# A hybrid attention and MLP block on one core: first MLP product by Strassen's rule in 256-token tiles, out-projection and second MLP product token-major

## What is computed

```python
x = x + merged @ w_out[layer]                 # 2048 x 2048
h2 = rms_norm(x, norm_mlp[layer])             # x * rsqrt(mean(x*x) + EPS) * gain
u = jax.nn.relu(h2 @ w_mlp_up[layer])         # 2048 x 8192
x = x + (u * u) @ w_mlp_down[layer]           # 8192 x 2048
```

## Time and profile before

| what | us |
|---|---|
| median of 3 runs | 2836.74 |
| lowest and highest run | 2836.65, 2838.22 |
| span of the profiled execution, first to last instruction | 2835.3 |
| PE busy in it | 2820.9 |
| DVE busy | 1366.4 |
| ACT busy | 898.5 |
| POOL busy | 39.7 |

### The profile page before, as it was taken

The page is one execution under the profiler, slowest core; times in us unless marked ns, Lnnn a source line. Parts: engine busy times, 40 slices in busy tenths (PEclk is TensorE's granted clock), DMA queues, the critical chain, the costliest instruction groups (busy, mean ns, idle before and its releaser), DMA issues.

```text
span 2835.3 us, 37750 instructions
## 1 busy us (share of the span) xinstructions
PE 2820.9 (99%) x12688; PEld 2307.9 (81%) x12688; DVE 1366.4 (48%) x2680; ACT 898.5 (32%) x1574; POOL 39.7 (1%) x66
## 2 busy tenths in 40 slices
PE   8999999999999999999999999999999999999999
PEld 7777787777888888878888888888888888888887
DVE  5666666666655555564444433343334433344332
ACT  5444444444322222233332222222222222222222
POOL 1000000000000000010000000000000000000000
PEclk9999999999999999999999999999999999999999
DMA  5222232222233333334433333333333333333342
GB/s 158 74 75 74 69 79 69 72 74 75 82 95 97 98 97 93 101 101 120 115 89 98 98 97 97 97 91 103 97 96 90 103 96 96 96 96 92 110 113 78
DMA packets 520798, 265.89 MB, mean 94 GB/s; under 512 B 8691, under 2 KB 518710, under 8 KB 520758
## 3 DMA queue, kind: packets, MB, share of 16 engines
q1 hardware_dynamic: 512198, 261.14, 32.7%
q10 hardware_dynamic: 8560, 4.23, 0.6%
HBM read 261.14 MB, written 4.19 MB: 94 GB/s over the span
## 4 chain that ended last, share of the span: by engine, by line
PE 99%; DVE 0%; DMA 0%; issue 0%; SPq 0%; ACT 0%; ACTq 0%
PE job L1107 31%; PE job L1110 31%; PE job L1109 31%; PE heads_out L1210 1%; PE scores L1153 1%; PE turned L1164 1%; PE stats L1118 1%; PE wide L1128 1%; PE scores L1146 1%; PE scores L1151 1%; DMA raw<-in_w_in 0%; PE turned L1364 0%; PE turned L1185 0%; PE wide L1444 0%; SPq L274 0%
## 5 line engine op out<-in xcount | busy, mean ns | idle before, releaser
L675 DVE TENSOR_TENSOR w_lo<-raw,w_hi 128x512 fp32r<-128x512 f32 x964 | 656.8, 689 | 902.3 <-ACT w_hi L411 901.4
L411 ACT ACTIVATE w_hi<-raw 128x512 fp32r<-128x512 f32 x964 | 606.3, 631 | 1421.7 <-PE job L1110 1419.3
L1107 PE MATMUL job<-a_hi,w_hi 128*128 128x512 f32 x2576 | 1023.2, 397 | 2.8 <-issue 2.0
L1110 PE MATMUL job<-a_hi,w_lo 128*128 128x512 f32 x2576 | 1005.0, 390 | 0.0
L1109 PE MATMUL job<-a_lo,w_hi 128*128 128x512 f32 x2576 | 1003.5, 390 | 0.0
L1107 PEld LDWEIGHTS job<-a_hi,w_hi 128*128 128x128 f32 x2576 | 483.9, 188 | 103.6 <-issue 5.1
L1110 PEld LDWEIGHTS job<-a_hi,w_lo 128*128 128x128 f32 x2576 | 483.6, 188 | 103.2
L1109 PEld LDWEIGHTS job<-a_lo,w_hi 128*128 128x128 f32 x2576 | 484.4, 188 | 95.3
L1107 PE MATMUL job<-b_hi,w_hi 128*128 128x512 f32 x1280 | 498.3, 389 | 0.0
L1110 PE MATMUL job<-b_hi,w_lo 128*128 128x512 f32 x1280 | 498.0, 389 | 0.0
L1109 PE MATMUL job<-b_lo,w_hi 128*128 128x512 f32 x1280 | 497.9, 389 | 0.0
(11 more groups left out here) (183 smaller groups left out, 1164.4 us busy)
## 6 DMA issues: line engine op xcount, KB each, us to landing
raw<-in_w_mlp_up SPq DMA_DIRECT2D x128, 512.0 KB, 4.0
raw<-in_w_mlp_down SPq DMA_DIRECT2D x128, 512.0 KB, 3.8
raw<-in_w_in SPq DMA_DIRECT2D x98, 512.0 KB, 3.9
raw<-in_w_gate SPq DMA_DIRECT2D x64, 512.0 KB, 4.0
raw<-in_w_out SPq DMA_DIRECT2D x32, 512.0 KB, 4.0
raw<-in_w_branch_diff SPq DMA_DIRECT2D x16, 512.0 KB, 3.8
raw<-in_w_branch_fox SPq DMA_DIRECT2D x16, 512.0 KB, 3.8
main<-in_x SPq DMA_DIRECT2D x16, 256.0 KB, 6.6
```

The source lines that it names most:

```text
L411: nc.scalar.activation(w_hi[:, u % SPLITS], raw[:, slot, part:part + KU], ACT.Copy).then_inc(hi_ready, 1)
L675: nc.vector.tensor_tensor(w_lo[:, u % SPLITS], raw[:, slot, part:part + KU], w_hi[:, u % SPLITS].bitcast(F32), ALU.subtract).then_inc(spli ...
L1107: nc.tensor.matmul(result[:, :], w_hi[:, slot, k], act_hi[:, f], start=(n == 0 and k == 0), stop=False)
L1110: done = nc.tensor.matmul(result[:, :], w_lo[:, slot, k], act_hi[:, f], start=False, stop=(n == units - 1 and k == KU - 1))
```

## The change

**Memory.** The buffers are laid out three times over the same space: once for all that comes before, a second time for the out-projection's end and the first MLP product, a third time for the second product. Two arrays in HBM are new: `u_rows` (8192 x 512, the squared activations) and `x2_rows` (the block's x after the out-projection).

**Out-projection, token-major** (`out_unit`, `add_x2`, `turn_x2`). The stationary operand is now a 128x128 tile of `a_hi`/`a_lo`, the streamed one 512 columns of w_out. The result has tokens on partitions. There are four blocks q of 512 output features (two strips of 256, one of each half of the features), each with 16 contraction blocks k, each with four token groups b and the three passes. The residual is loaded as it is and added without a transpose; ACT squares the sum with a running total for the norm and stores it to `x2_rows`; then PE turns it (16 transposes for each q) for the first MLP product. The norm's factor is not applied to it.

```
+            def out_unit(q, k):
+                ...
+                for b in range(TB):
+                    bank, rows = bank_sets[q % 2][b], slice(P * b, P * (b + 1))
+                    nc.tensor.matmul(bank[:, :], a_hi[:, k, rows], high, start=(k == 0), stop=False)
+                    nc.tensor.matmul(bank[:, :], a_lo[:, k, rows], high, start=False, stop=False)
+                    done = nc.tensor.matmul(bank[:, :], a_hi[:, k, rows], low, start=False, stop=(k == DT - 1))
+                done.then_inc(unit_used, 1)
+            def turn_x2(q):
+                pe.wait_ge(x2_added, 4 * q + 4)
+                for j in range(4):
+                    for b in range(TB):
+                        last = nc.tensor.transpose(bank_sets[q % 2][j][:, P * b:P * (b + 1)],
+                                                   x2_tok[:, b, P * j:P * (j + 1)], ident[:, :])
+                    last.then_inc(x2_turned, 1)
+            for q in range(BLOCKS):
+                for k in range(DT):
+                    if q > 0 and k == 3:
+                        turn_x2(q - 1)
+                    out_unit(q, k)
```

```
+            def up_unit(n, j, b, slices_wait=False):
+                pe.wait_ge(pair_lo_ready, n + 1)
+                for k in range(2):
+                    s = 2 * j + k
+                    if slices_wait:
+                        pe.wait_ge(h2_ready, s + 1)
+                    for a, w, bank, half in products:
+                        into = bank_sets[b][bank][:, 2 * P * half:2 * P * (half + 1)]
+                        high, low = pair_hi[j % 2][:, k, w], pair_lo[j % 2][:, k, w]
+                        nc.tensor.matmul(into, high, h_slices[s][:, a, 0], ...)
+                        nc.tensor.matmul(into, high, h_slices[s][:, a, 1], ...)
+                        done = nc.tensor.matmul(into, low, h_slices[s][:, a, 0], ...)
+                done.then_inc(pair_used, 1)
+            def sum_pair(n, j):                     # DVE
+                dve.wait_ge(pair_loaded[j], n * 8 + (32 - 8 * j))
+                nc.vector.tensor_tensor(t[:, :, 4:6], t[:, :, 1:3], t[:, :, 0:1].broadcast_to([P, 2, 2, P]), ALU.add)
+                dve.wait_ge(sums_first, n + 1)
+                nc.vector.tensor_tensor(t[:, :, 6], t[:, :, 4], t[:, :, 2], ALU.add)
+                dve.wait_ge(sums_second, n + 1)
+                nc.vector.tensor_tensor(t[:, :, 7], t[:, :, 6], t[:, :, 3], ALU.add)
+            def round_pair(n, j, ready):            # ACT
+                act.wait_ge(sums_ready, n + 1)
+                at_least(act, pair_used, ready)
+                nc.scalar.activation(pair_hi[j % 2], pairs[j][:, :, 1:8], ACT.Copy).then_inc(pair_hi_ready, 1)
+            def split_pair(n, j):                   # DVE
+                dve.wait_ge(pair_hi_ready, n + 1)
+                nc.vector.tensor_tensor(pair_lo[j % 2], pairs[j][:, :, 1:8], pair_hi[j % 2].bitcast(F32), ALU.subtract)
```

```
+                for b in range(TB):
+                    ...
+                    nc.vector.scalar_tensor_tensor(out_tok[:, t], bank_sets[c % 2][b][:, :], r2[:, t:t + 1],
+                                                   out_tok[:, t], ALU.mult, ALU.add).then_inc(out_ready, 1)
+                nc.tensor.matmul(bank[:, :], u_hi[slot][:, j % KU, rows], high, start=first, stop=False)
+                nc.tensor.matmul(bank[:, :], u_lo[slot][:, j % KU, rows], high, start=False, stop=False)
+                return nc.tensor.matmul(bank[:, :], u_hi[slot][:, j % KU, rows], low, start=False, stop=final)
```

More of the change, by code:

```diff
@@ new lines, in build @@
+        pairs = [pair_0, pair_1, pair_2, pair_3]
+        pair_hi = [t[:, 0:2 * 7 * P].rearrange("p (k i c) -> p k i c", k=2, i=7) for t in (hi_0, hi_1)]
+        pair_lo = [t[:, 0:2 * 7 * P].rearrange("p (k i c) -> p k i c", k=2, i=7) for t in (lo_0, lo_1)]
+        h_slices = [h_03[:, s] for s in range(4)] + [h_46[:, 0], h_57[:, 0], h_46[:, 1], h_57[:, 1]]
+        with ExitStack() as second:
+            u_out = over(second, "u_out", [P, 2, 2, S])
+            blocks = over(second, "blocks", [P, 8, 2 * P])
@@ L341, in _ @@
+            sp.wait_ge(pair_used, UPS - 2)
+            for c in range(BLOCKS):
+                down_loads(c, 0)
+                down_loads(c, 1)
+                load_back(c)
+                with sp.Fori(2, KD // (2 * KU)) as turn:
+                    down_loads(c, turn)
         @block.gpsimd
@@ L644, in _ @@
-            LAST = MLP.then((CH - 1) * CU + DT * JU, (CH - 1) * CJ + DT)
-            def last_down(m, work, j):
-                for u in range(JU):
-                    round_unit(work, u + LEAD)
-                    if u == 2 and not (isinstance(m, int) and m == 0):
-                        store(1 - j, m - 1)
-            last_down(0, LAST, 0)
-            for m in (1, 2):
-                last_down(m, LAST.then(m * JU, m), m % 2)
-            with act.Fori(1, DT // 2 - 1) as i:
-                work = Work(LAST.unit + JU, LAST.job + 1, i, 2 * JU, 2)
-                last_down(i * 2 + 1, work, 1)
-                last_down(i * 2 + 2, work.then(JU), 0)
@@ new lines, in up_pairs @@
+            def up_pairs(i, first=False, last=False):
+                for m in range(8):
+                    n = i * 8 + m
+                    if m == 1 and not first:
+                        copy_p1(i * 2 - 1, 1)
+                    if m == 5:
+                        copy_p1(i * 2, 0)
+                    if not (first and m < 4):
+                        round_pair(n, m % 4, n - 1)
+                    if m == 2 and not first:
+                        finish_pair(i * 2 - 1, 1)
+                    if m == 6:
+                        finish_pair(i * 2, 0)
```

754 lines of the change are left out of this document (470 added, 284 removed).

## The result

| | before | after |
|---|---|---|
| median, us | 2836.69 | 2784.66 |
| lowest and highest run, us | 2836.55, 2838.22 | 2784.0, 2785.91 |
| span of the profiled execution, us | 2835.3 | 2784.2 |
| ratio of the times | 1 | 0.9815, 95% interval 0.9801 to 0.9829 |

The change is 1.85% faster, 52.0 us. I had forecast 2746.5, 3.2% faster: the direction and the range held (2720 to 2795), and 38 of the 90 us did not come. In the traces the spans differ by 51.1 us.

A forecast was written before the change was run, and what follows sets the result against it. PE was taken as the bound, busy 2820.9 of 2835.3 us; -86.2 - 2.8 - 7.8 + 5.8 + 2.1 - 1.3 = -90.2 gave span 2745.1, median 2746.5 us, 3.2% faster. Range 2720 to 2795.

The forecast's parts named there:

- Part 1: First MLP product: 5376 matmuls of 256 columns at 113.5 ns replace 3072 of 512 at 226.7; -86.2 us.
- (a): First MLP product: the extra is fixed per matmul, 120.1 ns each; +35.5 us, 2782; chance 0.17.
- Does DVE keep up: First MLP product: DVE needs 16.2 of PE's 19.1 us per pair, combining unit just hidden; 0 us.
- Part 2: Out-projection: waits for the last tiles of `merged` go, -2.8 us, and 72 fewer transposes, -7.8 us.
- Late next is nothing: Out-projection: once the waits for `merged` go, no other wait follows, so the whole -2.8 us is gained.
- Part 3: Passage into the first MLP product: PE waits for first units and slices 6 and 7; +5.8 us (2 to 12).
- Part 4: Second product: same 3072 matmuls, loads asked for 17 us ahead, short waits at its start; +2.1 us (0 to 6).
- Part 5: End of the kernel: from the last matmul 4.0 us in place of 5.27; -1.3 us.
- (b): First MLP product: the weight load alone is the bound, 109 ns; 2726; counted with the forecast, together 0.60.
- (c): First MLP product: DVE becomes the bound, combining unit 0.9 us late at 20% over its prices; 2775; chance 0.08.
- (d): First MLP product: PE's sequencer at 62 ns per instruction makes 124 per matmul; +56 us, 2803; chance 0.05.
- (e): Each matmul of `up_unit`: weight loads are not hidden, 188 ns each; +400 us, 3147, or 3803; chance 0.08.

The follow-up runs named there:

- dve_more: Changed kernel with two more 128x512 DVE additions, results unused, ahead of the subtraction in each combining unit; 2822.93 us.
- tail: Changed kernel with the last three contraction blocks, not four, put token group by token group at the very end; 2782.86 us.
- eight256: Changed kernel with an eighth, unread product per slice in the first MLP product, 6144 matmuls of 256 columns in place of 5376; 2873.39 us.
- plain512: Changed kernel with the first MLP product's PE work put back to 3072 matmuls of 512 columns, all else as in the change; 2834.06 us.
- second probe: Changed kernel with first-product slices in other shapes (448 or 512 columns, 64 rows, 32 or 64 stationary columns, some narrower); matmul starts 59 to 230 ns apart.
- start: Changed kernel with the passage from out-projection into first MLP product reordered: first pair prepared earlier, slices 6 and 7 ahead of later pairs' sums; 2781.36 us.

## Why the prediction was right or wrong

**Part 1, the slot: wrong, and it is nearly the whole miss.** 120.0 ns against 113.5, 5376 x 6.5 ns = 34.9 of the 39.1 us. The bounds (109 and 120) held, and both ends turned out to be real: 110 is what 128-column loads allow, and 120 the matmul's cost. What failed is the choice between them. I wrote that 13.4 ns of each 512-column matmul are extra, and then halved that extra together with the columns ("the column rate of the MLP, 226.7 / 2"). No row asked for that. The two fp32r rows that could be asked, 0.31 less 0.19 in the earlier trace rows and 106.7 + 13.4, both said 0.12; what I held against them, the transposes' 2 ns, is float32 and has a different extra. So rival (a), which I gave 0.17, was the mechanism, and its 2782 stands 2.7 from the median. That the direction and the range held is owed to the bounds; the mechanism that I gave 0.60 was not the one at work. Split by the right rule, the trade reads: columns 655.4 to 573.4 us, -81.9; 2304 matmuls more at 13.4 ns, +30.9; together -51.

**Does DVE keep up: right.** L1249 takes 2.02 us (2.03). DVE is busy 493.78 of 620.20 us, 16.05 per pair of 20.16 where I had 16.2; the combining unit is ready 0.41 us before PE wants it. It is ready 4.62 us after the unit's start, so by this estimate it would have been just hidden in the forecast's unit of 4.77 too, as I had it. Experiment `dve_more` shows how thin that is.

**Part 2, out-projection: the sum near by luck, one step wrong.** 181.2 us against 185.2, where 180.7 were forecast. The transposes gave their 1.75 us; of the 2.8 us for waits only 1.4 came. The waits for the last tiles of `merged` are gone, but two for the weights' lo part take their place:

```profile
PE scores L1660 <- DVE w_lo L879: 1.2, 2, 0.9
```

"Late next is nothing" was the step that failed: the weights' subtractions stand behind the last ones of `merged` on DVE, and they were the next to be late: with restarting they cost 1.7 us. A term that the forecast did not have made up for it. A matmul of 512 columns that follows the transposes starts the next one after 0.31 to 0.32 us in place of 0.23; that happened 16 times before and 3 times now, 13 x 0.09 = 1.2 us.

**Part 3, the passage: +8.4 us for +5.8; the wait for slice 7 right (2.8 for 3.0), one step missed, one cost not priced.** Timeline of DVE and PE around the out-projection's end:

```profile
1420.08 2.03 DVE L1232 TENSOR_TENSOR h<-acts,h 128x1792 fp32r<-128x1792 f32 x1 [1.83 <-ACT h L739]
1422.02 0.69 DVE L1239 TENSOR_TENSOR pair<-pair 128x512 f32<-128x512 f32 x1
1423.65 3.53 ACT L745 ACTIVATE hi<-pair 128x1792 fp32r<-128x1792 f32 x2 [3.61 <-DVE pair L1244]
...
1425.06 0.39 PE L1662 MATMUL heads_out<-w_lo,a_hi 128*128 128x512 f32 x1
1425.46 2.03 DVE L1249 TENSOR_TENSOR lo<-pair,hi 128x1792 fp32r<-128x1792 f32 x1 [0.32 <-ACT hi L745]
1427.59 0.36 PE L1696 MATMUL scores<-h,hi 128*128 128x256 f32 x1 [2.14 <-issue]
...
1451.41 0.39 PE L1696 MATMUL scores<-h,hi 128*128 128x256 f32 x1 [2.59 <-DVE h L1232]
```

I had taken the first unit as ready when the out-projection ends. Its sums stand behind `split_acts(5)` on DVE, which ends at 1422.1; then come the sums, ACT's rounding and the subtraction, which ends at 1427.5, 2.3 us after PE wanted it (the profile calls it "issue", but the instruction that ended just then is L1249). Against that, no unit after the one with slice 7 was late.

The cost that I had not priced is the clock:

```profile
1425.30:1427.30 2.00, 0.15 (x1) 0.00 (x0) 1.84 (x1) 1.75 (x2) 0.00 (x0) 1.00 0.01 4
1428.90:1432.20 3.30, 3.30 (x17) 3.30 (x17) 3.30 (x4) 2.17 (x7) 0.00 (x0) 0.50 0.99 322
1452.80:1456.10 3.30, 3.30 (x17) 3.29 (x16) 3.23 (x5) 0.85 (x2) 0.00 (x0) 0.50 0.01 4
```

PE waits 2.3 and 2.8 us, works on at full clock for 1.3 and 1.4 us (from 1427.6 and 1451.4), and then the granted clock is 0.50 (1.2 GHz) for 3.4 us. In these 16 matmuls each time stand 213 ns apart in place of 120, 1.5 us. So the first wait of 2.3 us cost 3.8 in this execution.

**Part 4, second product: +3.6 for +2.1.** At its start 1.7 us of waits, where 1.4 and 0.7 had been expected. DMA at 201 GB/s and a share of 0.59 holds up nothing, though a load of 512 KB lands in 6.2 us, more than the 5.45 between two; being asked for 17 us ahead, as planned, covers that: after the start no wait of PE is for a load. What I missed is in the last block, where the order goes token by token: it needs the weights of the last four contraction blocks at once, while the block before them still holds one of the four slots:

```profile
2081.72 0.47 PE L1723 MATMUL scores<-w_hi_d,u_hi 128*128 128x512 f32 x1 [1.04 <-DVE w_lo_d L1339]
...
2767.72 0.39 PE L1725 MATMUL heads_out<-w_lo_d,u_hi 128*128 128x512 f32 x1
2769.61 0.50 PE L1723 MATMUL job<-w_hi_d,u_hi 128*128 128x512 f32 x1 [1.51 <-DVE w_lo_d L1339]
```

1.89 us where 0.23 would do: 1.7 lost, and `tail` gave back 1.8.

**Part 5, the end: right**, 3.8 us for 4.0:

```profile
2780.40 0.39 PE L1725 MATMUL heads_out<-w_lo_d,u_hi 128*128 128x512 f32 x1
2780.83 0.75 DVE L1357 SCALAR_TENSOR_TENSOR out_tok<-heads_out,r,out_tok 128x512 f32<-128x512 f32 x1 [1.97 <-PE heads_out L1725]
2781.61 0.34 ACTq L837 DMA_DIRECT2D out<-out_tok  x1
```

**The rivals.** (a) was it. (b) is a floor that exists, at 110, but not for 256 columns. (c) did not come about, and needs 0.4 us more per pair. (d) falls with the extra at 320 and 384 columns. (e) falls: at 120 ns no matmul waits for the recorded end (0.19) of a load.

## What to carry to other kernels

Measure the time of a matmul as columns at the clock plus a fixed part, in the type that is used, and price a change of tiling by both: here a rule that saves an eighth of the columns pays nearly four tenths of that back in 2304 matmuls more, and the half tile alone costs 39 us (`eight256` against `plain512`). Where two bounds are apart, take the value that rows of the same type and engine point to, not the middle. A helper engine at 80% can be the bound when its work is bunched: look at the one interval in which it has the most to do before PE's next wait.

## What the runs showed of the hardware that I had not expected

- Fp32r matmuls with fewer than 256 columns are not slower per column: 192 x 64 stationary takes 89 ns and 128 x 64 stationary 59. With 128 stationary columns both take 110, the time of the load.
- The fixed extra is 13 to 16 ns for fp32r with 128 stationary columns and 256 or more streamed ones, and 2 ns for float32 transposes. Float32 matmuls that are no transposes show the same: in the kernel before those of L1210 (near 146 us) stand 216, 322 and 428 ns apart at 256, 384 and 512 columns, which is two cycles of 2.4 GHz per column and 1 to 3 ns.
- Going from transposes back to fp32r matmuls costs some 0.09 us each time (0.31 to 0.32 for the first 512-column matmul in place of 0.227, before and after). Going from 128 rows to 64 costs more: in the second probe the last 128-row matmul and the first two with 64 rows stand 0.32 and 0.22 apart, and then 0.12.
- At 1.2 GHz the extra does not show: 256 columns are 213.3 ns, and the matmuls of the slow stretch of the changed kernel stand 0.21 apart, each of 0.41:

```profile
1429.27 0.41 PE L1696 MATMUL turned<-h,hi 128*128 128x256 f32 x1
1429.48 0.41 PE L1698 MATMUL turned<-h,hi 128*128 128x256 f32 x1
```

- The granted clock fell to one half for 3.4 us after PE had waited 2.3 and 2.8 us, in the changed kernel. With the same wait (listed as 2.14) at the same place, eight products of 256 kept the clock at 1.00:

```profile
1427.53 0.36 PE L1696 MATMUL scores<-h,hi 128*128 128x256 f32 x1 [2.14 <-issue]
...
1428.90:1432.20 3.30, 3.30 (x30) 3.30 (x29) 3.30 (x4) 2.15 (x6) 0.00 (x0) 1.00 0.96 320
```

  `tail`, which has the changed kernel's passage, kept the clock behind the first wait and lost it behind the second:

```profile
1428.00:1431.30 3.30, 3.30 (x30) 3.30 (x29) 3.30 (x5) 2.90 (x8) 0.00 (x0) 1.00 0.70 217
1450.90:1454.20 3.30, 3.30 (x18) 3.30 (x17) 3.23 (x5) 0.01 (x1) 0.00 (x0) 0.50 0.00 0
```

  So the same wait is followed by a fall in one execution and not in another. `start`, whose waits there were at most 1.09, kept the clock throughout. One profile of each is too little to say when it falls.
- The clock goes with most of the scatter. Each execution has a mean granted clock on record, rounded to three places. Of the 13 of the kernel before beside `plain512`, the six at 1.000 took 2836.37 to 2837.11 us and the seven at 0.999 took 2838.16 to 2838.6.
